# A third gate matrix by seven block products, in a stage of its own, in a hybrid decoder layer on one core

## The reference

```python
h = rms_norm(x, norm_mix_pre)
z = h @ w_in                       # 1024 x 10240, split into ten matrices of 1024 x 1024
a_h, a_b, a_c, c_a, c_g, s_u, s_v, g_a, g_c, g_s = split(z)
y_a = a_b * causal_dwconv(a_c * a_h, conv_a_w)                  # 3 taps
y_c = causal_dwconv(c_a * sigmoid(c_g), conf_dw_w) + conf_dw_b  # 31 taps
y_c = silu(layer_norm(y_c, conf_ln_g, conf_ln_b))
y_s = spatial_gating(gelu(s_u), gelu(s_v), ...)
merged = sigmoid(g_a) * (y_a @ w_branch[0]) + sigmoid(g_c) * (y_c @ w_branch[1]) \
       + sigmoid(g_s) * (y_s @ w_branch[2])
x = x + rms_norm(merged @ w_out, norm_mix_post)
f = square(relu(rms_norm(x, norm_ffn_pre) @ w_ff1)) @ w_ff2     # 1024 -> 4096 -> 1024
out = x + rms_norm(f, norm_ffn_post)
```

## Time and profile before

| what | us |
|---|---|
| median of 3 runs | 953.11 (953.0 to 953.18) |
| the profiled execution, its own time | 953.17 |
| its span, first to last instruction | 951.4 |
| PE busy | 942.3 |
| DVE busy | 718.3 |
| ACT busy | 431.9 |
| POOL busy | 102.6 |
| third gate stage, first matmul to that of the output projection | 495.66 to 582.92 |

### The profile page before, as it was taken

How to read it: one execution, slowest core, us unless ns; L and a number is a source line. 1 busy time by engine, 2 the same in 40 slices (tenths; PEclk the granted TensorE clock), 3 DMA queues, 4 the chain that set the end, 5 groups by cost and what they waited for, 6 DMA issues and landing times.

```text
span 951.4 us, 13452 instructions
## 1 busy us (share of the span) xinstructions
PE 942.3 (99%) x4823; PEld 807.2 (85%) x4823; DVE 718.3 (76%) x844; ACT 431.9 (45%) x537; POOL 102.6 (11%) x135
## 2 busy tenths in 40 slices
PE   9999999999999999999999999999999999999997
PEld 7888888888888888888888888899889989989985
DVE  5579879888888988886585444599875875786698
ACT  6543333233333322224374323377745745754774
POOL 1211001011100012222200000120001001100100
PEclk9999999999999999999999999999999999999999
DMA  8457558657765725554477323538586756858664
GB/s 313 146 161 228 168 174 229 184 193 192 190 192 177 199 89 132 132 135 151 134 187 255 111 90 110 199 128 239 164 256 126 239 164 159 230 139 239 186 192 131
DMA packets 41371, 168.01 MB, mean 177 GB/s; under 512 B 4968, under 2 KB 5360, under 8 KB 39024
## 3 DMA queue, kind: packets, MB, share of 16 engines
q1 hardware_dynamic: 31872, 111.85, 33.2%
q0 software_dynamic: 7680, 35.13, 21.1%
q10 hardware_dynamic: 1776, 20.45, 5.9%
HBM read 163.22 MB, written 37.75 MB: 211 GB/s over the span
## 4 chain that ended last, share of the span: by engine, by line
PE 97%; DVE 1%; DMA 1%; issue 0%; ACTq 0%; ACT 0%; DVEq 0%
PE ps L1631 26%; PE ps L1635 26%; PE ps L1633 26%; PE ps L1835 6%; PE ps L1837 6%; PE ps L1839 6%; PE ps L1713 1%; PE ps L1770 1%; DMA glu<-xt_in 1%; PE ps L1676 0%; DVE wide L1490 0%; DVE end L1478 0%; DVE wide L1473 0%; DVE w_lo L1111 0%; DVE end_a L1478 0%
## 5 line engine op out<-in xcount | busy, mean ns | idle before, releaser
L1111 DVE TENSOR_TENSOR w_lo<-raw,w_hi 128x1024 fp32r<-128x1024 f32 (+1 forms) x141 | 172.3, 1226 | 92.9 <-ACT w_hi L703 92.6
L703 ACT ACTIVATE w_hi<-raw 128x1024 fp32r<-128x1024 f32 (+1 forms) x140 | 146.0, 1052 | 200.9 <-PE ps L1635 118.0
L1631 PE MATMUL ps<-a_hi,w_hi 128*128 128x512 f32 x576 | 224.9, 390 | 0.0
L1635 PE MATMUL ps<-a_hi,w_lo 128*128 128x512 f32 x576 | 224.2, 389 | 0.0
L1633 PE MATMUL ps<-a_lo,w_hi 128*128 128x512 f32 x576 | 224.1, 389 | 0.0
L1199 DVE SCALAR_TENSOR_TENSOR conf<-glu,cols,conf (+1 forms) x240 | 186.6, 777 | 27.5 <-DVE conf L1199 26.4
L1635 PEld LDWEIGHTS ps<-a_hi,w_lo 128*128 128x128 f32 x576 | 108.1, 188 | 22.6
L1633 PEld LDWEIGHTS ps<-a_lo,w_hi 128*128 128x128 f32 x576 | 108.2, 188 | 22.2
L1631 PEld LDWEIGHTS ps<-a_hi,w_hi 128*128 128x128 f32 x576 | 108.2, 188 | 22.2
L1631 PE MATMUL ps<-w_hi,h_hi 128*128 128x512 f32 x224 | 87.2, 389 | 0.0
L1633 PE MATMUL ps<-w_lo,h_hi 128*128 128x512 f32 x224 | 87.2, 389 | 0.0
(11 more groups left out here) (188 smaller groups left out, 1576.3 us busy)
## 6 DMA issues: line engine op xcount, KB each, us to landing
raw<-units_in SPq DMA_DIRECT2D x127, 512.0 KB, 3.4
weight_sums<-units_in POOLq DMA_DIRECT2D x16, 1024.0 KB, 8.0
raw_v<-units_in SPq DMA_DIRECT2D x16, 512.0 KB, 6.1
glu<-units_in SPq DMA_DIRECT2D x16, 512.0 KB, 7.6
raw<-weight_sums SPq DMA_DIRECT2D x16, 512.0 KB, 4.2
glu<-units_in POOLq DMA_DIRECT2D x16, 512.0 KB, 5.4
raw_d<-units_in POOLq DMA_DIRECT2D x16, 512.0 KB, 6.8
glu<-weight_sums SPq DMA_DIRECT2D x8, 512.0 KB, 6.4
```

Source lines behind the costliest of these rows:

```text
L703: return nc.scalar.activation(dst, src, ACT.Copy, scale=scale)
L1111: return nc.vector.tensor_tensor(dst, src, hi, ALU.subtract)
L1631: nc.tensor.matmul(ps[:, bank, :], left_hi, right_hi, start=first, stop=False, skip_group_check=on_top)
L1635: return nc.tensor.matmul(ps[:, bank, :], left_lo, right_hi, start=False, stop=final, skip_group_check=on_top)
```

## The change

The gate matrix of the third gate and its branch matrix are no longer interleaved. The gate matrix comes first, as a stage of 14 units (`U_G`): seven block products in the order 1, 2, 4, 5, 3, 6, 7 with 256 columns a matmul. The branch matrix follows as 8 units (`U_B`) of 512 columns over four banks. The loads of weights still go through the two `raw` slots.

Four sums of gate weight blocks (products 5, 7, 6 and 4; 1 MB each) are made in DRAM during mixing, each by a copy and an accumulating DMA on POOL's queue (`g_sum`). Products 1, 2 and 4 take plain blocks of the normed x from `a_hi`, `a_lo`; the other four sets are differences. For these ACT stores the normed x (2 MB) to DRAM behind the eighth tile of it, DVE waits for that before it clears the pads, ACT reloads it in two halves of 1 MB (`load_xn`) over `conf`'s tiles as the SiLU work frees them, DVE makes the differences (`g_less`, `g_minus`), ACT and DVE their parts (`g_set_hi`, `g_set_lo`). Results are collected in `g_home` over `glu`: ACT copies a product out of its bank (`g_keep`), DVE adds later ones (`g_join`), ACT takes tanh (`g_gate`). The reload of x moves behind the high parts of the first branch units, the two rows behind the fourth branch unit. SP's load for the first product-5 sums of the MLP waits for the last `merged_ready` where it waited for `y_c_lo`.

The core of the diff (declarations, DRAM layout of the weights and the helpers' bodies are left out where the text above says what they do):

```diff
+U_G = U_GATE + 4 * KT
+G_UNITS = 14
+U_B = U_G + G_UNITS
+U_OUT = U_B + KT
 U_FF = U_OUT + KT
...
+G_BANK = {1: 0, 6: 0, 7: 0, 2: 4, 4: 6, 5: 2, 3: 2}
+G_ON_TOP = (6, 7, 3)
+G_SETS = {"22-21": 0, "11-21": 1, "21-22-11": 2, "21+12-11-22": 3}
...
+def g_unit(product, h):
+    return U_G + 2 * G_ORDER.index(product) + h
...
+            for product in G_ORDER:
+                for h in range(2):
+                    u = g_unit(product, h)
+                    sp.wait_ge(w_lo_ready, u - RAW + 1)
+                    if product in G_MADE:
+                        sp.wait_ge(g_summed[product], 32)
+                        sp.dma_start(raw[:, u % RAW, :], made_d[g_made(product) + h]
+                                     ).then_inc(raw_loaded[u % RAW], 16)
+                    else:
+                        load(g_block(PLAIN[product]) + h, u % RAW)
+            with sp.Fori(U_B // RAW, U_FF // RAW) as i:
+                for slot in range(RAW):
+                    sp.wait_ge(w_lo_ready, i * RAW + (slot - RAW + 1))
+                    load(i * RAW + (slot + D_B - U_B), slot)
...
+            def g_sum(product, step):
+
+                into = made_d[g_made(product):g_made(product) + 2].rearrange("h p n -> (h p) n")
+                if step == 0:
+                    at = g_block(G_FIRST[product])
+                    pool.dma_start(into, units_d[at:at + 2].rearrange("h p n -> (h p) n")
+                                   ).then_inc(g_summed[product], 16)
+                    return
+                pool.wait_ge(g_summed[product], 16)
+                if product in G_SOURCE:
+                    pool.wait_ge(g_summed[G_SOURCE[product]], 32)
+                    at = g_made(G_SOURCE[product])
+                    other = made_d[at:at + 2]
+                else:
+                    at = g_block(G_SECOND[product])
+                    other = units_d[at:at + 2]
+                pool.dma_start(into, other.rearrange("h p n -> (h p) n"), accum_op=ALU.add,
+                               max_dma_last_dim=SUM_BYTES).then_inc(g_summed[product], 16)
...
                 for k in ks:
                     act.wait_ge(xn_ready, k + 1)
                     copy_hi(a_hi[:, k, :], xt[:, k, :]).then_inc(act_hi_ready, 1)
+                if ks and ks[-1] == KT - 1:
+                    for t in range(2):
+                        act.dma_start(xn_d[t], xt[:, :, HALF_T * t:HALF_T * (t + 1)]).then_inc(xn_stored, 16)
...
+                if j == KT - 1:
+                    g_set_hi("22-21", 1)
+                    for h in range(2):
+                        g_done(1, h)
+                        g_behind(1, h)
+                    act.wait_ge(silu, KT)
+                    load_xn(1)
                 for t in SILU_TILES.get(j, ()):
                     act.wait_ge(silu, t + 1)
                     copy_hi(b_hi[:, t, :], nrm[:, t, :], 0.5).then_inc(y_c_hi, 1)
-
+                if j == KT - 2:
+                    load_xn(0)
+
+            for h in range(2):
+                g_done(2, h)
+                g_behind(2, h)
             act.wait_ge(y_c_lo, KT)
+            g_keep(1, "22")
+            g_done(4, 0)
+            g_behind(4, 0)
+            g_set_hi("21+12-11-22", 3)
+            g_done(4, 1)
+            g_behind(4, 1)
+            g_keep(4, "12")
+            g_set_hi("21-22-11", 2)
+            for h in range(2):
+                g_done(5, h)
+                g_keep(5, "11", h)
+                g_behind(5, h)
+            g_set_hi("11-21", 4)
+            g_done(3, 0)
+            g_behind(3, 0)
+            act.wait_ge(g_joined, 1)
+            g_gate("22", 1.0)
+            g_done(3, 1)
+            g_keep(3, "21")
+            g_behind(3, 1)
+            for h in range(2):
+                g_done(6, h)
+                g_behind(6, h)
+            act.wait_ge(g_lo_ready, len(G_SETS))
             act.dma_start(resid[:, :, :], x_d.rearrange("(c p) n -> p c n", p=P)).then_inc(x_again, 16)
...
+            act.wait_ge(g_joined, 3)
+            g_gate("21", -1.0)
+            for h in range(2):
+                g_done(7, h)
+                g_behind(7, h)
+            act.wait_ge(g_joined, 7)
+            g_gate("11", -1.0)
+            g_gate("12", 1.0)
+
+            for j in range(KT):
+                u = Count(U_B + j)
+                after(u)
+                split_hi(u.plus(RING))
+                act.wait_ge(merged_ready, KT + j + 1)
+                copy_hi(c_hi[:, j, :], merged[:, j, :], 0.5).then_inc(merged_hi, 1)
+                if j == CH - 1:
+                    for n, r in enumerate((ROW_MIX_POST, ROW_FFN_PRE)):
+                        act.dma_start(row[n], rows_d[r:r + 1, :].to_broadcast([P, D])).then_inc(rows_again, 16)
...
+                if j == KT - 1:
+                    dve.wait_ge(xn_loaded[0], 16)
+                    g_less("22-21", "22", "21")
                 for t in SILU_TILES.get(j, ()):
                     dve.wait_ge(silu_th, t + 1)
                     nc.vector.scalar_tensor_tensor(out=nrm[:, t, :], in0=conf[:, t, :], scalar=1.0,
                                                    in1=nrm[:, t, :], op0=ALU.add,
                                                    op1=ALU.mult).then_inc(silu, 1)
+                if j == KT - 1:
+                    g_set_lo("22-21", 1)
+                    for h in range(2):
+                        g_done(1, h)
+                        g_behind(1, h)
                 for t in SILU_TILES.get(j, ()):
                     dve.wait_ge(y_c_hi, t + 1)
                     lo(b_lo[:, t, :], nrm[:, t, :], b_hi[:, t, :], 0.5).then_inc(y_c_lo, 1)
 
...
+            g_done(2, 0)
+            g_behind(2, 0)
+            dve.wait_ge(xn_loaded[1], 16)
+            g_minus("21-22-11", "22-21", "11")
+            dve.wait_ge(g_diff, 2)
+            g_minus("21+12-11-22", "21-22-11", "12")
+            g_done(2, 1)
+            g_behind(2, 1)
+            g_set_lo("21+12-11-22", 2)
+            for h in range(2):
+                g_done(4, h)
+                g_behind(4, h)
+            dve.wait_ge(g_kept, 1)
+            g_join(2, "22")
+            g_less("11-21", "11", "21")
+            g_done(5, 0)
+            g_behind(5, 0)
+            g_set_lo("21-22-11", 3)
+            g_done(5, 1)
+            g_behind(5, 1)
+            g_set_lo("11-21", 4)
+            for h in range(2):
+                g_done(3, h)
+                g_behind(3, h)
+            dve.wait_ge(g_kept, 5)
+            for h in range(2):
+                g_done(6, h)
+                g_join(6, "21", h)
+                g_behind(6, h)
+            for h in range(2):
+                g_done(7, h)
+                g_join(7, "11", h)
+                g_join(7, "12", h)
+                g_behind(7, h)
+
+            for j in range(KT):
+                u = Count(U_B + j)
+                after(u)
+                if j == 0:
+                    dve.wait_ge(g_tanh, 4)
+                dve.wait_ge(merged_ready, KT + j)
+                nc.vector.scalar_tensor_tensor(out=y_a[:, :], in0=g_home[:, j, :], scalar=1.0,
+                                               in1=ps[:, 4 + j % 4, :], op0=ALU.add,
+                                               op1=ALU.mult).then_inc(gated, 1)
+                dve.wait_ge(gated, 2 * KT + j + 1)
+                nc.vector.tensor_tensor(merged[:, j, :], merged[:, j, :], y_a[:, :],
+                                        ALU.add).then_inc(merged_ready, 1)
+                split_lo(u.plus(RING))
+                dve.wait_ge(merged_hi, j + 1)
+                lo(c_lo[:, j, :], merged[:, j, :], c_hi[:, j, :], 0.5).then_inc(merged_lo, 1)
...
+            def g_bank_free(product, h):
+
+                if product == 3:
+                    pe.wait_ge(g_kept, 3 + h)
+                elif product == 6:
+                    pe.wait_ge(g_kept, 1)
+                elif product == 7:
+                    pe.wait_ge(g_joined, 2 + h)
+
+            for product in G_ORDER:
+                name = SET_OF[product]
+                again = product in G_ON_TOP
+                if name in G_SETS:
+                    pe.wait_ge(g_lo_ready, 1 + ("22-21", "21+12-11-22", "21-22-11", "11-21").index(name))
+                for h in range(2):
+                    u = g_unit(product, h)
+                    ready(Count(u))
+                    g_bank_free(product, h)
+                    for e in range(2):
+                        out = ps[:, G_BANK[product] + h, e * HALF_T:(e + 1) * HALF_T]
+                        free = again or e == 1
+                        for k in range(CH):
+                            w = slice((CH * e + k) * P, (CH * e + k + 1) * P)
+                            nc.tensor.matmul(out, w_hi[:, u % RING, w], gs_hi[name][:, k, :],
+                                             start=not free and k == 0, stop=False, skip_group_check=free)
+                            nc.tensor.matmul(out, w_hi[:, u % RING, w], gs_lo[name][:, k, :], start=False, stop=False,
```

(57 more changed lines are left out.)

67 lines of the change are left out of this document (58 added, 9 removed).

## The result

| | before | after |
|---|---|---|
| median of 5 runs each, us | 953.18 (953.0 to 953.66) | 957.7 (956.73 to 958.36) |
| ratio | 1 | 1.0044, 95% interval 1.0034 to 1.0055 |
| the profiled execution, us | 953.17 | 956.73 |
| its span | 951.4 | 955.0 |
| third gate stage, start to output projection | 87.26 | 90.68 |

The change makes the kernel 0.44% slower. The forecast of 955.9 us had the sign and the largest gap; the profiled execution is 0.8 us above it, the median 1.8.

The account below looks back on a forecast made before the run. PE was taken to bound the kernel, busy 99%. Replacing 43.5 us and 0.2 us of stall by 46.5 us (40.3 matmuls plus stalls 0.7, 0.7, 4.1, 0.7) took 953.17 to 955.9 us; range 952.5 to 960.0.

Parts of the forecast that it names:

- earlier stages pay: Rival: store and DRAM sums delay DVE or a load in the mixing stage; 1 to 3 us more, 957 to 959; chance 0.08.
- gaps ahead of 495 us: PE's timeline before the third gate stage: gaps there would show that the rival "earlier stages pay" holds.
- What is won: Gate matrix of the third gate: matmul time falls from 43.5 to 40.3 us, saving 3.2 us.
- Gaps ahead of G6 and G7: Gate-matrix units G6, G7 (of G0 to G13): late load, then set differences ahead of a low half; 0.7 us stall each.
- Gap ahead of G8: Gate-matrix unit G8 (of G0 to G13): PE waits for ACT's copy of product 5; 4.1 us stall.
- Gap ahead of G12: Gate-matrix unit G12 (of G0 to G13): PE waits for DVE's join behind G13's low half; 0.7 us stall.
- The sum: Gate-matrix stage: 40.3 + 0.7 + 0.7 + 4.1 + 0.7 = 46.5 us, against 43.5 + 0.2 before.
- the long order behind G7: ACT's program puts product 5's copy behind G9's high half, product 4's copy and a set's high half; 4.1 us stall.
- the round of two slots: Rival: gate-stage staging round 5.7 us for two units, PE eats them in 5.76; stage 49.3 to 49.6, time 959; chance 0.25.
- gaps ahead of every second unit released by low halves: PE's timeline in the gate stage: such gaps would show that the rival about the round of two slots holds.
- the one on which the sign hangs: PE's new wait ahead of G8 for ACT to copy out product 5's banks; 4.1 us.
- Elsewhere: Store of normed x, POOL's eight DMAs, moved reloads and a moved load: 0 each, bound +1 for the first two.

Follow-up runs that it names:

- e3_four_slots: Changed kernel with four staging slots instead of two from the gate stage's fifth unit on; 949.64 us median, ratio 0.9962 to the kernel before.
- e2_no_sets: Changed kernel without set work (no normed-x store or reload, differences or their halves; four products use a ready block); 953.36 us median, ratio 0.9998 to before.
- e7_pause_1: Kernel before plus one wait of PE for one POOL operation ahead of the third gate stage's third unit; 954.79 us median, ratio 1.0014.
- e1_copy_early: Changed kernel with ACT's two copies of product 5 moved ahead of high halves that wait for loads; 958.18 us median, ratio 1.0052 to before.
- e6: Changed kernel with three staging slots instead of two from the gate stage's fifth unit on; 950.63 us median, ratio 0.9971 to the kernel before.
- e8_pause_2: Kernel before plus one wait of PE for two POOL operations in a row ahead of the third gate stage's third unit; 956.73 us median, ratio 1.0032.
- e5_no_sets_late_sum: e2_no_sets with POOL's last accumulating sum for the MLP moved from the gate stage's start to behind the first branch unit; 952.1 us median, ratio 0.9985.

## Why the prediction was right, and where it was off

The profiled execution, 956.73 us, lies where the prediction had its own forecast (955.0 to 957.5). The median of 957.7 lies just above that, in the 957 to 959 of the rival "earlier stages pay", whose sign, gaps ahead of 495 us, is not in the trace.

- *What is won* was right: 192 matmuls of 0.2267 us against 336 of 0.120. With the waits gone (e3_four_slots) gate and branch units take 83.9 us where they took 87.26: the 3.2 us and the 0.2 of stall. The median gains 3.7. The neighbouring stage of the same shape priced it. The Trainium skill ("TensorE: Matmul & The Clock Gate", Back-to-back issue gap) has 215.8 and 109.2 ns by its isolated formula and a sustained 131 ns for 512 columns. Measured were 226.7 ns and 120 ns, so neither rate holds in this kernel.
- *Gaps ahead of G6 and G7*: 0.7 and 0.7 forecast, 0.60 and 0.49 measured. At G6 two misses cancel, and that is luck. ACT was held by the SiLU tiles until 503.94, 8.1 us into the stage and not 6.7, because the high half ahead of them waited for G3's load:

```profile
497.41 1.06 ACT L794 ACTIVATE w_hi<-raw 128x1024 fp32r<-128x1024 f32 x1 [4.03 <-DMA raw<-units_in]
```

  That load took 8.9 us beside the first reload of the normed x, and 7.1 in e2_no_sets, which has no such reload. So G6's load went 1.1 us later than forecast, and then took 3.3 us where the forecast allowed 5.3.
- *Gap ahead of G8*: 4.1 forecast, 3.91 measured, with the releaser that was named. Laying the two engines' programs in order against the earlier trace rows gave this to 0.2 us.
- *Gap ahead of G12*: 0.7 forecast, 0 measured. The join ended at 536.03, 0.5 us earlier in the stage than forecast, and PE came to G12 only at 537.2, held up by the half clock of the next point. Without that it would have been there at 535.7 and waited 0.3 (an estimate).
- *The half clock* is the term that was missing: 1.5 us in the profiled execution. The sum took 0.120 us for every matmul of the stage. That the stage came out only 0.6 us above the 46.5 forecast is in part luck, since the 0.7 at G12 did not come. It makes most of what the profiled execution lies above the sum: 40.3 + 0.6 + 0.5 + 3.9 + 1.5 = 46.8 of 47.13 us, and 0.15 us of later start; 0.3 us are spread over small waits. The median is another 1.0 us higher. The runs at 957.7 to 958.4 have a mean clock of 0.995 against 0.996 and 0.997 of the two at 956.7, which would fit more of the same. But that mean says little: e7_pause_1 has 0.997 in the execution whose profile shows the full clock at its gap, e1_copy_early 0.999. No trace shows the cause of this 1.0 us.
- *Why the gaps are there* was half right. The prediction placed the cause in the long order behind G7 and, as a rival with a chance of 0.25, in the round of two slots, which it put at 5.7 us for two units, against PE's 5.76, with no reserve. The bare round is that (5.63 to 5.75 us in the first three rounds of e2_no_sets), but it grows to 6.6 where a landed load waits for ACT's other work. Of the 6.8 us that after loses over pace, 3.1 are there with two slots and no set work, 1.5 are the clock, and the remaining 2.2, by difference, come with the set work. None of it is left in the profiled executions with a third slot (e6) or a fourth (e3). So the rival was nearer to the cause than its chance of 0.25, though its sign, gaps ahead of every second unit released by low halves, was not what the trace showed. The early copy (e1) took away two thirds of the wait that the prediction called the one on which the sign hangs, and the time did not fall.
- *Elsewhere*: the store, the eight DMAs on POOL's queue and the moved reloads cost nothing that the trace shows ahead of the stage or behind it: 0.15 us at 495 us, and 0 behind 586. The stage starts between 495.17 and 496.10 in the profiles of before, after and e1 to e6, so 0.15 is no difference. What the first reload of the normed x cost inside the stage stands under G6.

## What to carry to other kernels

When PE's units get shorter, count the round of a staging slot (load, high half, low half, and what stands before each on its engine) against the units it must feed. Here the bare round was 5.7 us against 5.76, so there was nothing in reserve for a slow load or for other work ahead of a high half, and one slot more took every gap out of the profiled execution. A wait that a profile names with its releaser is where a lack surfaces, not always its cause: check by moving it, and see whether another appears further on. A gap in a busy PE can cost more than its length: here those of 3.9 us (after) and 2.5 us (e8_pause_2) cost some 1.5 us on top in the profiled executions, those of 2.1 us (e1_copy_early) and 1.3 us (e7_pause_1) did not.

## What was not expected of the hardware

In this kernel a stretch of half clock followed a still PE of 3.75 us, and one of 2.29 us in the profiled execution of e8_pause_2. That kernel's eight runs lie in two groups of four, 1.4 us apart; the profiled one is of the upper. Behind a still PE of 1.96 us in the profiled execution of e1_copy_early, and of 1.18 us in that of e7_pause_1, the clock stayed full. The fall came within 1 us after work had been taken up again, and the lower level stayed for about 3.4 us both times.

Two loads of 512 KB issued 1.1 us apart took 5.0 and 5.1 us in one execution (e5_no_sets_late_sum, at 504.60 and 505.74). Another such pair took 3.3 and 4.4 (e3_four_slots, at 516.25 and 517.39). Why they differ is not shown.
